# Reading the decode states out over four column strips of the PE array in a hybrid retention and sliding-window trunk

## The reference, cut to what matters

```python
def retention(h, s0, pos, w_in, w_out):
    """S_t = gamma S_{t-1} + k_t^T v_t, o_t = q_t S_t (exact chunkwise form)."""
    ...
    def step(S, xs):
        qi, ki, vi = xs
        cross = jnp.einsum('bihd,bhde->bihe', qi * q_dec[None, :, :, None], S)
        S = S * c_dec[None, :, None, None] + jnp.einsum('bjhd,bjhe->bhde', ki * k_dec[None, :, :, None], vi)
        return S, cross
    ...
    o = (intra + cross.transpose(1, 0, 2, 3, 4)).reshape(B, T, H, dv)
    o = o * lax.rsqrt(jnp.mean(o * o, axis=-1, keepdims=True) + EPS)
    o = o.reshape(B, T, H * dv) * jax.nn.silu(g)
    return o.astype(h.dtype) @ w_out, s_fin
```

## Time and profile before

| | |
|---|---|
| time, median of 3 runs | 3052.37 us (3050.44 to 3052.54) |
| profiled execution, span from first to last instruction | 3050.0 us |
| around the span, by the median of the runs | 2.4 us |
| PE busy | 2976.0 us, 98% |
| DVE busy | 1262.6 us, 41% |
| ACT busy | 742.6 us, 24% |
| DMA | 174.5 MB, mean 57 GB/s |

### The profile page before, as it was taken

How to read it: one execution, slowest core, us unless ns; L and a number is a source line. 1 busy time by engine, 2 the same in 40 slices (tenths; PEclk the granted TensorE clock), 3 DMA queues, 4 the chain that set the end, 5 groups by cost and what they waited for, 6 DMA issues and landing times.

```text
span 3050.0 us, 42635 instructions
## 1 busy us (share of the span) xinstructions
PE 2976.0 (98%) x17496; PEld 2777.9 (91%) x17496; DVE 1262.6 (41%) x1638; ACT 742.6 (24%) x1318; POOL 163.7 (5%) x78
## 2 busy tenths in 40 slices
PE   7999999999999999999999999899899999999999
PEld 7879959968986999999999999689679999999999
DVE  6443443443344633233332355744764233332333
ACT  3131132123123322111222131531553111222111
POOL 2000000000000200000000021211220000000000
PEclk9999999999999999999999999899899999999999
DMA  3122041122213111111111122103001111111111
GB/s 126 64 102 63 29 137 62 45 87 77 64 49 114 42 49 46 45 45 45 45 45 45 45 71 57 45 18 102 19 18 49 46 45 45 45 45 45 45 48 74
DMA packets 91333, 174.50 MB, mean 57 GB/s; under 512 B 9840, under 2 KB 15344, under 8 KB 90416
## 3 DMA queue, kind: packets, MB, share of 16 engines
q1 hardware_dynamic: 89296, 167.40, 17.1%
q10 hardware_dynamic: 1920, 5.41, 0.8%
HBM read 143.83 MB, written 25.56 MB: 56 GB/s over the span
## 4 chain that ended last, share of the span: by engine, by line
PE 92%; DVE 5%; ACT 2%; issue 1%; DMA 0%; ACTq 0%; SPq 0%; DVEq 0%
PE ps L1133 78%; PE ps L1298 2%; PE ps L1275 2%; PE ps L1470 2%; PE ps L1270 2%; PE ps L1444 1%; DVE wlo L701 1%; PE ps L1281 1%; PE ps L1173 1%; PE ps L1457 1%; PE ps L1304 1%; DVE x L738 1%; DVE hlo L708 1%; PE ps L1243 1%; ACT sq L477 1%
## 5 line engine op out<-in xcount | busy, mean ns | idle before, releaser
L1133 PE MATMUL ps<-hhi,whi 128*128 128x352 f32 x2976 | 651.0, 327 | 25.8 <-DVE hlo L708 16.3
L1133 PE MATMUL ps<-hhi,wlo 128*128 128x352 f32 x2976 | 643.5, 324 | 0.0
L1133 PE MATMUL ps<-hlo,whi 128*128 128x352 f32 x2976 | 643.0, 324 | 0.0
L468 ACT CAST whi<-wraw 128x512 fp32r<-128x512 f32 x424 | 261.1, 618 | 1135.2 <-PE ps L1133 1121.7
L701 DVE TENSOR_TENSOR wlo<-wraw,whi 128x512 fp32r<-128x512 f32 x424 | 333.9, 794 | 486.9 <-ACT whi L468 486.9
L1133 PEld LDWEIGHTS ps<-hhi,whi 128*128 128x128 f32 x2976 | 506.9, 190 | 29.7 <-DVE hlo L708 17.8
L1133 PEld LDWEIGHTS ps<-hhi,wlo 128*128 128x128 f32 x2976 | 512.7, 188 | 0.0
L1133 PEld LDWEIGHTS ps<-hlo,whi 128*128 128x128 f32 x2976 | 507.8, 189 | 0.0
L1133 PE MATMUL ps<-ahi,whi 128*128 128x352 f32 x2112 | 460.6, 326 | 9.1 <-DVE alo L1111 6.3
L1133 PE MATMUL ps<-ahi,wlo 128*128 128x352 f32 x2112 | 456.0, 323 | 0.0
L1133 PE MATMUL ps<-alo,whi 128*128 128x352 f32 x2112 | 455.3, 324 | 0.0
(11 more groups left out here) (156 smaller groups left out, 1925.0 us busy)
## 6 DMA issues: line engine op xcount, KB each, us to landing
wraw<-in_weights SPq DMA_DIRECT2D x424, 256.0 KB, 2.6
s<-in_state_in SPq DMA_DIRECT2D x32, 512.0 KB, 3.7
out_state_s<-s SPq DMA_DIRECT2D x32, 512.0 KB, 2.8
zr<-z_a ACTq DMA_DIRECT2D x40, 132.0 KB, 2.4
x<-in_xT SPq DMA_DIRECT2D x8, 528.0 KB, 8.7
rope_tab<-in_tables SPq DMA_DIRECT2D x4, 1056.0 KB, 4.8
out_yT<-x SPq DMA_DIRECT2D x8, 528.0 KB, 2.6
atab<-in_attn_tables SPq DMA_DIRECT2D x2, 1056.0 KB, 5.2
```

Of the source, the lines that this page charges most:

```text
L468: act.copy(whi[:, i % RING, :], wraw[:, i % RING, :]).then_inc(w_hi, 1)
L1133: mm = pe.matmul(ps[:, 3 * (m % 2) + t, 0:TB], a[:, slot, w], b[:, s * KG + k, t * TB:(t + 1) * TB], start=(first and j == 0), stop=(last ...
```

## The change

The read-out's two matmuls of 512 columns become four of 256: value columns in two halves, and for each the two halves j of the key features. Each of the four writes its own 32 partitions of bank 7, that is, its own strip of 32 columns of the array. The three new strips start their own sums with the first sequence; the first strip still goes on from `sample_within`. At the head's end DVE joins the strips: it copies three of them out, adds them in the right columns and leaves the sum in `k_tok` (with `sc_t` as spare room), from where ACT's `norm_o` reads it for the decode tokens instead of from bank 7. ACT waits for the new semaphore `o_sum`, twice counted per head.

```diff
@@ norm_o (ACT)
                 rows = NS if c == CH else P
-                bank = 7 if c == CH else 2 + c % 2
-                act.wait_ge(o_done, i + 1)
+                if c == CH:
+                    act.wait_ge(o_sum, 2 * h + 2)
+                    out = o_smp
+                else:
+                    act.wait_ge(o_done, i + 1)
+                    out = ps[:, 2 + c % 2, :]
...
-                act.activation(o_tok[0:rows, :], ps[0:rows, bank, :], ACT.Square, scale=qdec,
+                act.activation(o_tok[0:rows, :], out, ACT.Square, scale=qdec,
...
-                act.mul(o_tok[0:rows, :], ps[0:rows, bank, :], stat[0:rows, 3:4]).then_inc(o_kept, 1)
+                act.mul(o_tok[0:rows, :], out, stat[0:rows, 3:4]).then_inc(o_kept, 1)
@@ new on DVE, called after the eighth update_sample
+            def join_sample(h):
+
+                dve.wait_ge(o_done, (h + 1) * (CH + 1))
+                dve.tensor_copy(k_tok[0:NS, 0, :], ps[NS:2 * NS, 7, 0:DK]).then_inc(dve_seq, 1)
+                dve.tensor_copy(k_tok[0:NS, 1, :], ps[2 * NS:3 * NS, 7, DK:DV]).then_inc(dve_seq, 1)
+                seq[0] += 2
+                spare = sc_t[0:NS, :, :].rearrange("p j f -> p (j f)")
+                link(h, dve.tensor_copy(spare, ps[3 * NS:4 * NS, 7, DK:DV]))
+                dve.tensor_tensor(k_tok[0:NS, 0, :], ps[0:NS, 7, 0:DK], k_tok[0:NS, 0, :], ALU.add).then_inc(o_sum, 1)
+                link(h, dve.tensor_tensor(k_tok[0:NS, 1, :], ps[0:NS, 7, DK:DV], k_tok[0:NS, 1, :], ALU.add))
+                dve.tensor_tensor(k_tok[0:NS, 1, :], spare, k_tok[0:NS, 1, :], ALU.add).then_inc(o_sum, 1)
...
                     update_sample(h, c)
+                join_sample(h)
                 inverse_rms(h, CH)
@@ sample_head (PE)
-                for j in range(2):
-                    mm = pe.matmul(ps[0:NS, 7, :], q_sel[:, b % 2, j, :], s0[:, b % S0_RING, j, :],
-                                   start=False, stop=(b == NB - 1 and j == 1))
+                for half in range(2):
+                    for j in range(2):
+                        rows = slice(NS * (2 * half + j), NS * (2 * half + j + 1))
+                        cols = slice(half * DK, (half + 1) * DK)
+                        mm = pe.matmul(ps[rows, 7, cols], q_sel[:, b % 2, j, :], s0[:, b % S0_RING, j, cols],
+                                       start=(b == 0 and half + j > 0), stop=(b == NB - 1))
```

More of the change, by code:

```diff
@@ L132, in trunk @@
         o_tok = at("o_tok", o_r + 7168, [P, DV], F32)
+        o_smp = k_tok[0:NS, :, :].rearrange("p j f -> p (j f)")
         hmask = at("hmask", o_r + 9216, [P, P + NS], F32)
@@ L224, in trunk @@
         o_kept = sem("o_kept")
+        o_sum = sem("o_sum")
         ot_done = sem("ot_done")
@@ L744, in _ @@
                     split(0, -LEAD + 1 + k, -LEAD + 2 + k)
-            N_SEQ = 12 + (CH + 1) + 3 + 2 + NB
+            N_SEQ = 12 + (CH + 1) + 3 + 2 + NB + 4
             seq = [0]
```

## The result

The changed kernel takes 3025.99 us in the median of 4 runs (3019.79 to 3027.33), the kernel before 3052.09 in the same comparison: a ratio of 0.9914 with a 95% interval of 0.9902 to 0.9927, 26.1 us less. The prediction was 3033, with a range of 3029 to 3055. The direction was right and the gain larger than the range allowed.

A forecast was written before the change was run, and what follows sets the result against it. PE, busy 98% of the span, was taken to bound the kernel through its order in the chunk loop. 32 read-outs at -0.60 us and 4 joins at 0 sum to -19.3: 3052.4 becomes 3033, range 3029 to 3055.

The forecast's parts named there:

- The reading of the bound: Chunk loop: PE's order decides; one step is 7.89 us, of which the read-out takes 1.83.
- Nothing else ends last inside the loop: Chunk loop: in a step's chain, matmul stages follow each other on PE with no other engine between them; step 7.89 us.
- The split alone gains nothing: Read-out: eight shorter instructions one after another take 1.84 us, the 1.83 of before.
- (c): Read-out: strips overlap but instructions start in order, five slots, 1.19 to 1.27 us, 0.60 less taken; chance 0.55.
- (b): Rival, read-out: all four strips run together, two slots, 0.54 us, 1.29 less per step, time 3015; chance 0.07.
- The room on DVE: Loop step: DVE is free 0.93 us before L800; at most about 0.12 of a 1.29 gain lost.
- the prediction's own signs of being wrong: Among them: steps shorten by less than the read-out does, meaning DVE took over, L800 first.
- no piece but L800's successor in the chain: Head's end: chain has no other DVE or ACT piece; turn_o follows product 8's first slab without a wait.
- The join: Head's end on DVE: three copies, three additions, at most 2.6 us, covered by product 8's first slab, cost 0.
- The rival that each change of strip drains the array: Read-out: three moves between strips add 0.33 to 0.51 us, time 3063 to 3069 without overlap; chance 0.14.

The follow-up runs named there:

- one strip: From the kernel before: read-out in four matmuls of 256 columns, all on the first strip, no join; 3055.81 us, ratio 1.0016.
- two split strips: Changed kernel with one strip per key-feature half, each in two matmuls of 256 columns, the first strip's both first; 3027.88 us, measured once.
- update first: Changed kernel with DVE's decode-state update ahead of its reciprocal of the norm in all steps but the last; 3016.71 us, ratio 0.989.
- no join: Changed kernel without its six DVE join instructions, ACT reading the first strip alone, output incomplete; 3024.4 us, ratio 0.9914.
- the two with the loop moved: Changed kernel with 128 satisfied waits starting PE's program, 3019.81 us; the same plus DVE's update ahead of its reciprocal, 3010.43 us.
- two strips unsplit: Changed kernel with one strip per key-feature half, each one matmul of 512 columns, join shortened; 3028.34 us, ratio 0.9927.

## Why the prediction was wrong

The reading of the bound was right for the steps in the middle: PE's order decided there, and most of what the read-out lost came off the time. "Nothing else ends last inside the loop" was not right of the last step, where L800 on DVE ended last already before. "The split alone gains nothing" was right (1.84 forecast and measured, on one strip).

The step that failed is (c), "strips overlap, but instructions start in their order": B1 does not wait behind A2. Each strip works off its own instructions, so the eight fill two slots (0.57) instead of five (1.19 to 1.27). I saw the program's order A1 A2 B1 B2, and took an order for starting from it that no row of before showed. Two rules of "TensorE: Matmul & The Clock Gate" (Part 3, Trainium skill) that I weighed come out differently: the one that matmuls of different strips run at the same time agrees with the trace (four starts within 30 ns, some 7 apart where the page has some 4), the one that all matmuls start in program order does not, when it is read across strips. The sentence of the same part that a weight load overlaps a running matmul only on other rows, taken by itself, does not hold here either: on two split strips the eight loads lie from 410.25 to 410.83, beside matmuls on the same 128 rows that start at 410.26.

With (b) in place of (c) my own sum said 3015, and the time is 3026, so that sum had two more wrong terms. *The room on DVE*: at most 0.12 of a step's gain was to be lost again, and some 0.22 was. That the update on DVE would show first was among the prediction's own signs of being wrong. I counted the 0.24 between the end of L800 and the start of L1275's matmul as cover. The row that I left out, in the same timeline of before:

```profile
407.61 0.31 PEld L1275 LDWEIGHTS ps<-v_tok,k_tok 128*128 128x128 f32 x2 [0.55 <-issue]
```

The weight load starts 0.12 after L800 ends (407.49), exactly as it does after the change, where the matmul starts 0.15 after L806's end. So most of the 0.24 is the signal and the load, and little of it is room. The update now starts 0.29 after the increment on PE has ended (408.00 against 407.71), where it was 0.03: 0.26 later, and 0.23 of that shows. And I took the room from one step in the middle, so that the first step (ACT's table load, 2.9 us) and the last (chunk 7's norm, 1.8 us) were not seen; both could have been read from the timeline of before. At the loop's end the prediction wanted no piece but L800's successor in the chain, and chunk 7's norm on ACT stands there. *The code*: 64 more instructions on PE per head were taken to cost only their own time; with them each jump has a second stall, and that cost 5.7 us, the lower clock included.

That the time lies only 7 us from 3033 is in part luck, since the errors have opposite signs: the read-outs gave 32 x 0.66 = 21 us more than (c) said, and 9.9 in the loops and 5.7 at the jumps were lost that the sum did not have.

The join was right in its parts: 402 to 424 ns each against 0.42, done 2.58 us after L806 against at most 2.6, and ACT's result 1.1 us before the turn needed it, against 1.2. DVE and ACT at the end of the loop in head 1:

```profile
429.18 0.42 DVE L843 COPY k_tok<-ps 32x256 f32<-32x256 f32 x1
...
431.31 0.41 DVE L850 TENSOR_TENSOR k_tok<-sc_t,k_tok 32x256 f32<-32x256 f32 x1
...
433.30 0.72 ACT L531 ACTIVATE o_tok<-k_tok,stat 32x512 f32<-32x512 f32 x1
```

L531 ends at 434.02, and the turn's weight loads start at 435.09. What is late is what the prediction named, and it was covered; the run without the join shows the same time.

The rival that each change of strip drains the array fell: seven further instructions on four strips fit into 0.57 us. That agrees with "TensorEngine Tiling (Array Packing)" of the Trainium skill, Key Properties, by which a change of mode drains and a change of tile does not.

## What to carry to other kernels

Where a stationary operand has only 32 columns, giving neighbouring matmuls different strips of 32 output partitions lets them share the time of one: 1.83 us went to 0.98 with two strips and to 0.57 with four, and two strips did it in both orders of the instructions that were run. Two strips without a second split are most of it when other engines leave little room (24.8 of the 30.4 us in the loops here). When such an operation gets shorter, look at each step of its loop, the first and the last too, for the wait that ends next to it, and don't count the gap between a producer's end and the matmul's start as cover, since the signal and the weight load lie in it. Here turning round two operations on DVE was worth another 9 us.

## What the runs showed that was not expected

Strips run apart from one another even for f32 operands, which take two instructions for each matmul (eight in the trace for four), and with all 128 rows in use. The place of a loop in PE's code is worth 4 to 6 us in this kernel (3.8 around the jumps with the update first, 5.9 in the change, where the clock fell too): the four kernels with as many PE instructions in the loop as the change (one strip, two split strips, no join, update first) have a second stall too, in the chain as a piece of 1.18 to 1.72 us behind a few matmuls; the two with the loop moved, and two strips unsplit, which has as many PE instructions as before, have one. A comparison of kernels that differ by a few instructions can be off by that much.
